# A two-block transformer forward pass on one core: the order of the first stage's loads and sums, and of four kinds of work in the first mixer and the expert stage

## What is computed

```python
# first block
mod = silu(c) @ w_ada + b_ada                      # 6 x 1024 values
h = rmsnorm(x, norm1_g) * (1 + mod[1]) + mod[0]
proj = h @ w_in                                    # queries, keys, values, gates of two mixers
o1 = hgrn2_mixer(...)                              # gated linear recurrence, 4 heads
o2 = nsa_mixer(...)                                # attention: compressed, selected, window branches
x = x + mod[2] * (concat(o1, o2) @ w_out)
h = rmsnorm(x, norm2_g) * (1 + mod[4]) + mod[3]
x = x + mod[5] * (routed_experts(h) + swiglu(h, w_sh_gu, w_sh_dn))
# second block, two layers: feed-forward, mixer, feed-forward, with mod of c_2 @ w_mod
```

## Time and profile before

| | |
|---|---|
| time, median of 3 runs | 3089.05 us (3085.66 to 3092.69) |
| the profiled execution's own time | 3091.34 us |
| its span in the trace | 3089.5 us |
| mean granted TensorE clock | 0.986 of full speed |
| PE busy, share of the span | 96% |
| DVE / ACT / POOL busy | 53% / 37% / 9% |

### The profile page before, as it was taken

How to read it: one execution, slowest core, us unless ns; L and a number is a source line. 1 busy time by engine, 2 the same in 40 slices (tenths; PEclk the granted TensorE clock), 3 DMA queues, 4 the chain that set the end, 5 groups by cost and what they waited for, 6 DMA issues and landing times. The chain is left out here.

```text
span 3089.5 us, 38761 instructions
## 1 busy us (share of the span) xinstructions
PE 2967.4 (96%) x13952; PEld 2311.7 (75%) x13952; DVE 1647.4 (53%) x1773; ACT 1149.2 (37%) x1355; POOL 262.8 (9%) x425
## 2 busy tenths in 40 slices
PE   6998898999999998999999999999999999999998
PEld 4886665777676766888877778887888877778886
DVE  6745846666666656555346565523655246543322
ACT  4123624666666653222225432212222125432211
POOL 0100001222222220000000000000000000000000
PEclk9989999999999999999999999999999999999999
DMA  7543226999999996554222155422544222122221
GB/s 287 167 157 123 83 75 242 360 351 362 371 353 351 356 314 267 204 190 163 95 99 73 64 191 190 177 95 70 209 177 172 94 106 75 69 95 95 95 95 68
DMA packets 115276, 554.59 MB, mean 180 GB/s; under 512 B 20593, under 2 KB 22130, under 8 KB 72946
## 3 DMA queue, kind: packets, MB, share of 16 engines
q1 hardware_dynamic: 88690, 490.39, 43.3%
q0 software_dynamic: 26496, 62.96, 5.8%
HBM read 548.06 MB, written 37.75 MB: 190 GB/s over the span
## 5 line engine op out<-in xcount | busy, mean ns | idle before, releaser
L181 ACT ACTIVATE stream_high<-stream_raw 128x2048 fp32r<-128x2048 f32 x151 | 289.2, 1916 | 801.4 <-PE ffn_ps_psum L571 756.7
L186 DVE TENSOR_TENSOR stream_low<-stream_raw,stream_high 128x2048 fp32r<-128x2048 f32 x156 | 356.6, 2287 | 406.7 <-ACT stream_high L181 406.2
L569 PE MATMUL ffn_ps_psum<-h_high_f,stream_high 128*128 128x512 f32 x1344 | 525.0, 391 | 0.0
L571 PE MATMUL ffn_ps_psum<-h_high_f,stream_low 128*128 128x512 f32 x1344 | 523.1, 389 | 0.0
L570 PE MATMUL ffn_ps_psum<-h_low_f,stream_high 128*128 128x512 f32 x1344 | 522.9, 389 | 0.0
L324 DVE TENSOR_TENSOR expert_low<-expert_raw,expert_high 128x2048 fp32r<-128x2048 f32 x128 | 293.3, 2292 | 223.1 <-ACT expert_high L320 216.2
L571 PEld LDWEIGHTS ffn_ps_psum<-h_high_f,stream_low 128*128 128x128 f32 x1344 | 252.3, 188 | 52.7
L570 PEld LDWEIGHTS ffn_ps_psum<-h_low_f,stream_high 128*128 128x128 f32 x1344 | 252.4, 188 | 52.3 <-issue 0.2
L569 PEld LDWEIGHTS ffn_ps_psum<-h_high_f,stream_high 128*128 128x128 f32 x1344 | 252.3, 188 | 52.2 <-issue 0.2
L320 ACT ACTIVATE expert_high<-expert_raw 128x2048 fp32r<-128x2048 f32 x128 | 244.2, 1908 | 118.0 <-PE experts_g_psum L571 113.2
L803 DVE TENSOR_TENSOR ffn_sg<-ffn_sg,ffn_ps_psum 128x512 f32<-128x512 f32 x88 | 60.5, 687 | 414.6 <-PE ffn_ps_psum L571 410.6
(11 more groups left out here) (491 smaller groups left out, 4566.0 us busy)
## 6 DMA issues: line engine op xcount, KB each, us to landing
expert_raw<-in_exp_gu SPq DMA_DIRECT2D x128, 1024.0 KB, 11.9
stream_raw<-in_ffn_gu SPq DMA_DIRECT2D x88, 1024.0 KB, 4.8
expert_raw<-in_exp_dn SPq DMA_DIRECT2D x64, 1024.0 KB, 7.6
con<-in_w_mod SPq DMA_DIRECT2D x120, 512.0 KB, 5.5
stream_raw<-in_ffn_dn SPq DMA_DIRECT2D x44, 1024.0 KB, 4.9
mix_mod_rows<-in_w_ada POOLq DMA_DIRECT2D x32, 512.0 KB, 4.8
stream_raw<-in_w_in SPq DMA_DIRECT2D x16, 1024.0 KB, 4.9
pieces_raw<-in_w_in SPq DMA_DIRECT2D x13, 1024.0 KB, 6.1
```

What stands on the lines that cost most here:

```text
L181: self.nc.scalar.activation(self.high[:, q], self.raw[:, q], ACT.Copy).then_inc(self.high_done, 1)
L186: self.nc.vector.tensor_tensor(self.low[:, q], self.raw[:, q], self.high[:, q].bitcast(F32), ALU.subtract)\
L569: mm(out, w[0], x[0], start=start, stop=False)
L571: return mm(out, w[1], x[0], start=False, stop=stop)
```

## The change

**First stage.** Piece 0 is loaded ahead of x. Rows 4 to 7 are loaded as eight halves of 512 KB, the four of the first chunk first, and summed as eight operations of 1024 columns. ACT makes piece 0's high part before the squares, DVE its low part before rows 4 to 7. PE gets four products of the vectors (428 columns) once row 3 is there, whose result is overwritten. The split of piece 1 leaves the stage: ACT makes its high part in the mixer behind the eight `h_high`, DVE its low part behind the eight `h_low`.

**First mixer.** The split of piece 18 moves from item 1 to behind the items (on ACT to item 24, ahead of the last copy), `mod_c`'s rows go to the other raw slot, and pieces 19 and 20 are loaded after the last row of `mod_c`, piece 20 after piece 18's split. On DVE the four `recurrent` move from items 15 to 18, where they stood ahead of `scale`, to items 11, 13, 15, 16, behind it; `recurrent_low` from 17 to 20 to 13, 15, 17, 18. Four of `mod_d`'s eight sums move ahead of the last `out_to_low`.

**Expert stage.** The DVE product `hid` moves from ahead of the adds of j = 4 to ahead of those of j = 3.

```diff
@@ first stage, SP, ACT, DVE, PE
-                    for k in range(SLOTS):
-                        rows(k)
-                    sp.dma_start(self.xT[:], t["xT"].rearrange("(n p) t -> p n t", p=P)).then_inc(x_loaded, 16)
-                    for k in range(SLOTS, KD):
-                        rows(k)
-                    for n in range(2):
-                        w.load(sp, n, n, next_w[n])
+                    w.load(sp, 0, 0, next_w[0])
                     sp.dma_start(self.xT[:], t["xT"].rearrange("(n p) t -> p n t", p=P)).then_inc(x_loaded, 16)
+                    for g in range(2):
+                        for k in range(SLOTS, KD):
+                            if g == 0:
+                                sp.wait_ge(summed, k - SLOTS + 1)
...
+                    w.load(sp, 1, 1, next_w[1])
...
+                    w.split_high(act, 0, 0)
                     act.wait_ge(x_loaded, 16)
...
-                    w.split_high(act, 0, 0)
                     act.wait_ge(ones_done, 2)
                     root.root(act)
-                    w.split_high(act, 0, 1)
...
                     root.before(dve)
-                    w.split_low(dve, 0, 1)
...
+                    pe.wait_ge(loaded[SLOTS - 1], 16)
+                    for _ in range(4):
+                        nc.tensor.matmul(ps[:, 0, 0:NVEC], self.ones[:], self.vec[:], start=True, stop=True)
                     root.sum_each(pe)
@@ first mixer
+            RECURRENT = (11, 13, 15, 16)
...
-                    for n in range(8, ALL - 1):
+                    for n in range(8, ALL - 2):
                         load(n)
                     sp.wait_ge(mod_c.summed, KD + mod_c.slots)
-                    load(ALL - 1)
+                    for n in range(ALL - 2, ALL):
+                        load(n)
...
-                    pool.wait_ge(w.low_done, OUT + 2)
+                    pool.wait_ge(w.low_done, OUT + 1)
                     mod_c.load(pool, 0, range(KD))
...
                     norm.vector(dve)
+                    w.split_low(dve, 0, 1)
...
-                        if 15 <= i < 19:
-                            recurrent(i - 15)
-                        if 17 <= i < 21:
-                            recurrent_low(i - 17)
                         if i:
                             scale(i - 1)
-                        if i == 1:
-                            split(18)
+                        if i in RECURRENT:
+                            recurrent(RECURRENT.index(i))
+                        if i - 2 in RECURRENT:
+                            recurrent_low(RECURRENT.index(i - 2))
...
+                    split(18)
+                    mod_d.multiply(dve, 0, range(KD // 2))
                     out_to_low(0)
-                    mod_d.multiply(dve, 0, range(KD))
+                    mod_d.multiply(dve, 0, range(KD // 2, KD))
@@ expert stage
                     for j in range(1, 5):
-                        if j == 4:
+                        if j == 3:
                             dve.wait_ge(up_done, 2)
```

More of the change, by code:

```diff
@@ L461, in start @@
             e, s2, z, pos = (self.sb(x, [P, 4]) for x in "e s2 z pos".split())
-            loaded = [self.sem(f"loaded{s}") for s in range(SLOTS)]
+            loaded, halves = [self.sem(f"loaded{s}") for s in range(SLOTS)], [self.sem(f"half{n}") for n in range(2 * SLOTS)]
             (vec_loaded, x_loaded, ones_done, there, c_ready, abs_done, lb_sub, lb_done, chain_s, summed, turned) = self.sems(
@@ L468, in _ @@
                 def _(sp):
-                    def rows(k):
-                        if k >= SLOTS:
-                            sp.wait_ge(summed, k - SLOTS + 1)
-                        sp.dma_start(wk[:, k % SLOTS], t["w_ada"][0:2, k * P:(k + 1) * P, :].rearrange("a p n -> p a n"))\
-                            .then_inc(loaded[k % SLOTS], 16)
                     sp.dma_start(self.vec[:], t["vecs"]).then_inc(vec_loaded, 16)
                     for k in range(SLOTS):
-                        rows(k)
+                        sp.dma_start(wk[:, k], t["w_ada"][0:2, k * P:(k + 1) * P, :].rearrange("a p n -> p a n")).then_inc(loaded[k], 16)
+                    w.load(sp, 0, 0, next_w[0])
                     sp.dma_start(self.xT[:], t["xT"].rearrange("(n p) t -> p n t", p=P)).then_inc(x_loaded, 16)
-                    for k in range(SLOTS, KD):
-                        rows(k)
-                    for n in range(2):
-                        w.load(sp, n, n, next_w[n])
+                    for g in range(2):
+                        for k in range(SLOTS, KD):
+                            if g == 0:
+                                sp.wait_ge(summed, k - SLOTS + 1)
+                            sp.dma_start(wk[:, k - SLOTS, g, :], t["w_ada"][g:g + 1, k * P:(k + 1) * P, :].rearrange("a p n -> (a p) n"))\
+                                .then_inc(halves[SLOTS * g + k - SLOTS], 16)
+                    w.load(sp, 1, 1, next_w[1])
                 @block.gpsimd
@@ L529, in rows @@
                     def rows(k, a, b):
-                        dve.wait_ge(loaded[k % SLOTS], 16 * (k // SLOTS + 1))
                         x = wk[:, k % SLOTS, a:b, :]
@@ L534, in rows @@
                         else:
-                            dve.wait_ge(summed, k)
+                            dve.wait_ge(summed, k if k < SLOTS else k + SLOTS * a)
                             v.scalar_tensor_tensor(out=acc[:, a:b, :], in0=x, scalar=ca[:, k:k + 1], in1=acc[:, a:b, :],
                                                    op0=ALU.mult, op1=ALU.add).then_inc(summed, 1)
-                    for k in range(KD - 1):
+                    for k in range(SLOTS):
+                        dve.wait_ge(loaded[k], 16)
                         rows(k, 0, 2)
-                    rows(KD - 1, 0, 1)
-                    rows(KD - 1, 1, 2)
                     w.split_low(dve, 0, 0)
+                    for g in range(2):
+                        for k in range(SLOTS, KD):
+                            dve.wait_ge(halves[SLOTS * g + k - SLOTS], 16)
+                            rows(k, g, g + 1)
                     dve.wait_ge(turned, 1)
@@ L550, in _ @@
                     pe.wait_ge(ones_done, 2)
+                    pe.wait_ge(vec_loaded, 16)
+                    pe.wait_ge(loaded[SLOTS - 1], 16)
+                    for _ in range(4):
+                        nc.tensor.matmul(ps[:, 0, 0:NVEC], self.ones[:], self.vec[:], start=True, stop=True)
                     root.sum_each(pe)
@@ L553, in _ @@
                         if i % 8 == 0:
-                            pe.wait_ge(summed, KD + i // 8)
+                            pe.wait_ge(summed, KD + SLOTS * (i // 8))
                         mm = nc.tensor.matmul(ps[:, 0, i:i + 1], acc[:, i // 8, (i % 8) * P:(i % 8 + 1) * P], self.ones[:, 0:1],
@@ L951, in first_mixer @@
             mod_c = Modulation(self, t["w_mod"], 1, self.v("c_2"), self.v("b_mod"), self.mod_all[:], bank(MISC),
[L952 removed]
+                               w.raw[:, (OUT + 2) % 2].rearrange("p (s n) -> p s n", s=2), 2, mod_rows[:, 0, :], "c")
             mod_d = Modulation(self, t["w_mod"], 2, self.v("c_2"), self.v("b_mod"), self.mod_all[:], bank(out_bank[1]),
@@ L1373, in _ @@
                     norm.scalar(act)
+                    w.split_high(act, 0, 1)
                     mod_a.start(act)
@@ L1477, in _ @@
                             exponents(i)
-                        if i == 1:
-                            split(18, place(25) + 1)
-                        elif 6 <= i < 14:
+                        if 6 <= i < 14:
                             if i % 2 == 0:
@@ L1488, in _ @@
                                 a(at[:, hd, :], at[:, hd, :], ACT.Exp, scale=-0.5).then_inc(rooted, 1)
-                        if 16 <= i < 20:
-                            hd = i - 16
+                        if i - 1 in RECURRENT:
+                            hd = RECURRENT.index(i - 1)
                             act.wait_ge(hg_out, hd + 1)
@@ L1494, in _ @@
                             copy(i - 2)
+                        if i == ITEMS:
+                            split(18, place(25) + 1)
                     out_to_high(0)
```

2 lines of the change are left out of this document (removed).

## The result

The changed kernel takes 3074.37 us in the median of 5 runs (3071.74 to 3080.55), the kernel before 3090.0 beside it (5 runs): a ratio of 0.9949, with a 95% interval of 0.9935 to 0.9964. It is 15.6 us faster by these medians; the forecast was 3075, in a range of 3068 to 3083. Eight more runs of the changed kernel, among the experiments, had a median of 3080.28 and a ratio of 0.9967 (0.9955 to 0.9978). Over all 13 its mean is 3077.7, against 3089.6 over 72 runs of the kernel before: 11.9 us, with an interval of about 9.5 to 14.4 by resampling. That is the number to explain. The runs of the experiments come from three chips, so each kernel is also set against the kernel before as it ran beside it: by that the first five runs of the changed kernel lead by 15.0 us and the eight later ones by 11.5, 12.8 over all 13. The first five were on the lucky side.

A forecast was written before the change was run, and what follows sets the result against it. PE, busy 96% of the span, was taken as the bound, with time to win only where it waits or runs at half clock. Terms 1.1 + 6.2 + 2.0 + 5.0 = 14.3 from 3089.05 gave 3074.8, say 3075; range 3068 to 3083.

The forecast's parts named there:

- upper bound of 19.5: Whole kernel: largest total gain in us from the bounds of the terms, taken from 3089.05 to give 3069.5.
- First stage, forecast 1.1: First stage: the mixer's first product starts earlier, a gain of 1.1 us, from -0.2 to 4.0.
- rival (a): First stage: the new products keep PE's clock up, gaining 4.0 us instead of 1.2; total 3072, chance 0.12.
- The rows are no bound: First stage: last row lands at 32.9 and is added by 34.2, just when the sum of squares ends.
- Rival (d): First stage: four additional transfers paid one behind the other, 8 us later, stage -6.9; total 3083, chance 0.03.
- Item 1's split, forecast 6.2: Attention items 1 and 2: without the split PE starts 4.7 us earlier, plus 1.5 from full clock; 4.7 to 6.5.
- Rival (b): Attention items: the ring of waiting engines takes back half of 6.2 + 2.0 us; total 3079, chance 0.14.
- Recurrence, forecast 2.0: Attention items 11 to 20: moving DVE work from its full stretch to free time gains 2.0 us, 0 to 3.5.
- Expert stage, forecast 5.0: End of expert stage: earlier `hid` lets PE start turning 5.0 us sooner, 3.9 if it waits for a transfer.
- Rival (c): Expert stage: later rows from memory come too late, gaining 1 us instead of 5.0; total 3079, chance 0.07.
- (e): Attention items: a denser, finer-grained PE falls to half clock; six more such items make it slower, chance 0.03.
- (f): Whole kernel: no gain reaches the end because a later stage waits for something unmoved; total 3089, chance 0.06.

The follow-up runs named there:

- experiment 10: Kernel before the change with only the new first stage added; median 3091.45 us over 12 runs, ratio 1.0004.
- experiment 11: Changed kernel with `recurrent` at items 15 to 18 behind `scale` and `hid` ahead of the last add of j = 2; median 3074.11 us, ratio 0.9949.
- experiment 5: Changed kernel without the four products of the vectors ahead of the sum of squares; median 3077.9 us over 6 runs, ratio 0.9959.
- experiment 6: Changed kernel with nine instead of four products of the vectors ahead of the sum of squares; median 3076.38 us over 6 runs, ratio 0.9953.
- experiment 4: Changed kernel with the whole first stage as before, piece 1 split in it again; median 3077.62 us over 8 runs, ratio 0.9963.
- experiment 2: Changed kernel with the split of piece 18 back at item 1; median 3082.59 us over 12 runs, ratio 0.998.
- experiment 7: Changed kernel with `recurrent` at the old items 15 to 18, but behind `scale`; median 3075.13 us over 6 runs, ratio 0.9946.
- experiment 1: Changed kernel with the DVE recurrence where it was, items 15 to 18 ahead of `scale`; median 3073.54 us over 12 runs, ratio 0.9960.
- experiment 3: Changed kernel with the DVE product `hid` back ahead of the adds of j = 4; median 3081.32 us over 12 runs, ratio 0.9981.
- experiment 8: Changed kernel run again, unchanged; median 3080.28 us over 8 runs, ratio 0.9967 against the kernel before.

## Why the prediction was right, and where it was not

**The total** came out near the forecast by two large terms whose mechanism it had right (6.2 and 5.0), while a term of 2.0 had the wrong sign and was partly made up by two gains that it had put too low. By the traces' stretches the terms are: first stage 1.8 (41.1 less the mean start of 39.3 in the eight traces that have the new stage with four products), items 0 to 4 6.4 to 6.65, recurrence -1.4 to -2.0 (means of all traces: 43.3 in six with the old items, 44.7 in seven with the new; the low end holds two long ones, experiments 10 and 11), expert stage 6.9 (48.3, the mean of four traces with `hid` at j = 4, less 41.4, that of eight with j = 3). The sum is some 13 to 14, beside a measured 11.9 (12.8 by the lead) and a forecast of 14.3. That the median of the first five runs, 3074.4, fell within 1 us of the 3075 is luck twice over: those runs were below their kernel's mean, and the errors of the terms cancel. The prediction's upper bound of 19.5 isn't the sum of its terms either: 4.0 + 6.5 + 3.5 + 5.0 is 19.0, and the expert stage had been given no upper bound, though its term was the one that came out above.

**First stage, forecast 1.1.** The start of the mixer moved by 0.5 to 2.8 us, around that value. The sum of squares started at 25.16 (24.9 forecast), and the four products left PE at half clock when it began (a mean granted clock of 0.57 from 24 to 28 us): rival (a) falls, since without them (experiment 5) and with nine (6) the mixer starts at 38.30 and 39.90, within the 38.3 to 40.6 of the traces with four. "The rows are no bound" was wrong: the prediction let the last half row land at 32.9 and be added by 34.2. It landed at 33.3, but DVE, with each half costing it 1.38 us where the transfers bring one in 1.28, was done at 35.39, and PE's second half of the turning stands behind it. Of the earlier start no clear gain shows in the times (experiments 4 and 10); whether it is lost again to the clock or lies under the noise stays open. Rival (d), in which the four additional transfers would be paid one behind the other, 8 us, falls with this window over the halves:

```profile
24.00:34.00 10.00, 8.85 (x22) 4.19 (x22) 8.99 (x7) 4.94 (x10) 0.00 (x0) 0.83 1.00 402
```

The queue moved 402 GB/s with 512 KB transfers at a DMA share of 1.00, and the last half landed at 33.3 where the last row had landed at about 30.4: 2.9 us later, of which the one 1 MB transfer put ahead takes 2.5. The Trainium skill (DMA: Bandwidth & Descriptors, "Anatomy of one DMA") gives a fixed part of about 2.0 us for one transfer that GpSimd issues; these are SP's, and whatever fixed part they have overlaps here.

**Item 1's split, forecast 6.2.** Right in each step: the idle time 4.77 to 0.67, the transposes 1.94 to 1.06, the clock at 1.00. From score(3) to those transposes PE gained 4.6 us (4.7 forecast), from there to score(4) 1.75 (1.5 forecast); measured 6.38 in the profiled pair and 6.65 by experiment 2. Rival (b), that the ring takes half back, falls for this term. Behind the items piece 18 costs nothing: DVE's split ends at 383.95, some 7 us ahead of PE's first need.

**Recurrence, forecast 2.0: this step failed.** The prediction said "it is the bound there" of DVE in items 15 to 20, from 26.60 busy of 28.87 us. Taking 3.85 us off the stretch behind it left that as long as it was (experiment 7): DVE had filled with the recurrence time in which it would have waited for PE's scores and ACT's high part, 5.9 us instead of 1.8. By the prediction's own cut, items 15 to 20, the stretch from score(15) to score(21) did not shrink by 3.5 but grew, from 29.0 us (experiments 1 and 7) to 29.8 to 30.1 in six of the seven traces with the new items. The overflow in front was the right idea: put at 1.4 for items 11 to 14, it is 0.9 there (16.9 against 16.0 from score(11) to score(15)) and another 0.5 at item 16, 1.4 together over items 13 to 16. The term is thus -1.6 at the same clocks and -2.0 in most traces, below the bounds of 0 to 3.5. This is rival (b) after all, but for the recurrence alone, and worse than it was priced.

**Expert stage, forecast 5.0.** Right mechanism, sized too low: 5.5 in the profiled pair and 6.9 over the traces; experiment 3 lost 6.5 of the lead. The first trace of before was the shortest of the four with `hid` at j = 4 (47.42 against 48.15 to 49.09), and the forecast took its rows. Rival (c) falls: turning follows `shared_down` with no idle time.

**Rivals (e) and (f).** Items 4 to 13, the denser ones by the split's move, take 38.25 to 38.27 us in all traces but one (38.63, with the old items), so (e) falls for them. In small it came true for the recurrence: in five of the seven traces with the new items, and in none of the six with the old, the clock fell to half within items 13 to 16, which took 17.2 us there instead of 15.7; items 17 to 22 were 1.2 us shorter in four of these five, so some 0.3 of it is left. The prediction had named a clock "at half where it was at full" as a sign of being wrong, and for this term it was. (f) falls by the times of experiments 2 and 3: put back, each part costs 6 to 7 us of the lead, some 5 by the plain means.

## What to carry to other kernels

Busy time near 90% doesn't make an engine the bound of a ring: where three engines wait for each other, read which wait ends last in each item, and treat work that stands in such waits as free until a window without it has shown otherwise. Filling another stretch's free time past the brim costs the overflow. Cutting a transfer in two also cuts the operation behind it in two: look whether the engine that takes the halves (1.38 us each here) still keeps up with the queue that brings them (1.28). When a kernel's runs spread over 0.4% with its granted clock (3070.4 us at a mean of 0.990, 3083.5 at 0.987), one profiled pair can show 20 us where 12 are real; compare the same stretch over several traces before you explain a difference in it.

## What the chip showed that was not expected

From identical code up to that point, the mixer's first product started at 38.3 to 38.8 us in some executions and at 40.4 to 40.6 in others, by how much of the sum and the turning ran at half clock (8.53 and 3.87 us in the profile after, 9.68 and 4.57 in experiment 8). The projections took 227.7 to 238.2 us with a granted clock of 0.97 to 0.93, with no change in what PE had to do there. And though PE had worked through eighteen passes ahead of the sum of squares and then at full clock, the 16 passes behind a wait of 1.48 us took 3.58 us instead of 1.84 (experiment 6).
